# A hybrid decoder trunk: indexer score products placed between the weight products of the second recurrent projection chunk, and every selection round placed in the gaps of VectorE

## What is computed

```python
h = rms_norm(x, norm_g[l])
proj = h @ w_in[l]
a_part, b_part, c_part, gate_part = split_cols(proj, ...)
o_a = dsa_mixer(a_q, a_k, a_v, a_qi, a_ki, a_wi, bias_a)      # top-k attention
o_b = gated_deltanet_mixer(b_qkv, b_a, b_b, conv_w, ...)      # recurrent
o_c = nsa_mixer(c_q, c_kv, c_g, ...)                          # compressed, selected, window
merged = g_a * (y_a @ wb_a) + g_b * (y_b @ wb_b) + g_c * (y_c @ wb_c)
x = x + merged @ w_out[l]
```

```python
idx_logits = jnp.einsum('bqhd,bsd->bqhs', qib, k_idx) * (IDX_DIM ** -0.5)       # IDX_HEADS = 8, IDX_DIM = 64
score = jnp.einsum('bqh,bqhs->bqs', wb * (IDX_HEADS ** -0.5), jax.nn.relu(idx_logits))
score = jnp.where(key_pos[None, None, :] <= t[None, :, None], score, NEG_INF)
_, sel = lax.top_k(score, topk)                                                 # topk = 128
```

## Time and profile before

| | us |
|---|---|
| median of 3 runs | 659.43 (658.7 to 665.79) |
| the profiled execution, its own time | 658.73 |
| its span (first to last instruction) | 656.9 |
| mean granted TensorE clock | 0.982 of full |

### The profile page before, as it was taken

The page is one execution under the profiler, slowest core; times in us unless marked ns, Lnnn a source line. Parts: engine busy times, 40 slices in busy tenths (PEclk is TensorE's granted clock), DMA queues, the critical chain, the costliest instruction groups (busy, mean ns, idle before and its releaser), DMA issues.

```text
span 656.9 us, 9683 instructions
## 1 busy us (share of the span) xinstructions
PE 606.8 (92%) x3643; PEld 383.7 (58%) x3643; DVE 372.4 (57%) x820; ACT 324.5 (49%) x565; POOL 222.3 (34%) x161
## 2 busy tenths in 40 slices
PE   3869999999999997999999899999999999899998
PEld 2424557655347754777677677655666677333443
DVE  6401485443799989887878757342324453577411
ACT  4535645336656857622613415445766767243510
POOL 0133453522016466222630521226431233142520
PEclk9998999999999899999999999979999999899999
DMA  9244775543013332120210210202031111162411
GB/s 320 62 124 112 157 112 168 155 134 112 2 33 101 110 97 65 32 65 1 78 52 1 65 32 1 77 21 62 8 94 32 66 65 33 32 221 74 145 59 48
DMA packets 31167, 53.03 MB, mean 81 GB/s; under 512 B 2743, under 2 KB 13201, under 8 KB 31121
## 3 DMA queue, kind: packets, MB, share of 16 engines
q1 hardware_dynamic: 30961, 52.27, 27.8%
q10 hardware_dynamic: 160, 0.14, 0.1%
HBM read 49.98 MB, written 2.42 MB: 80 GB/s over the span
## 4 chain that ended last, share of the span: by engine, by line
PE 67%; DVE 17%; ACT 4%; issue 4%; POOL 3%; DMA 2%; SPq 2%; DVEq 0%; ACTq 0%; POOLq 0%
PE bank L1510 11%; PE bank L1512 10%; PE bank L1511 10%; PE bank L1682 8%; PE bank L1750 5%; PE bank L1752 5%; PE bank L1754 5%; DVE work L1246 3%; PE bank L1858 3%; DMA stage<-in_w_in 2%; PE bank L1546 2%; POOL w_lo L500 2%; DVE early L1154 2%; PE bank L1666 2%; PE bank L1877 2%
## 5 line engine op out<-in xcount | busy, mean ns | idle before, releaser
L500 POOL TENSOR_TENSOR w_lo<-stage,w_hi 128x1024 f16<-128x1024 f32 (+4 forms) x76 | 149.8, 1973 | 243.1 <-ACT w_hi L713 243.1
L1682 PEld LDWEIGHTS bank<-work 128*128 128x128 f32 x616 | 75.3, 192 | 17.6 <-DVEq L1221 12.5
L1682 PE MATMUL bank<-work 128*128 128x128 f32 x616 | 79.8, 278 | 5.5 <-DVEq L1221 5.1
L713 ACT ACTIVATE w_hi<-stage 128x1024 f16<-128x1024 f32 (+4 forms) x76 | 74.5, 981 | 16.8 <-issue 12.4
L705 ACT ACTIVATE stage<-stage,small 128x512 f32<-128x512 f32 (+4 forms) x120 | 73.6, 662 | 7.7 <-DMA stage<-in_w_in 7.7
L1750 PE MATMUL bank<-hT_hi,w_hi 128*128 128x512 f16 x192 | 74.5, 388 | 1.7 <-PE bank L1754 0.9
L1752 PE MATMUL bank<-hT_lo,w_hi 128*128 128x512 f16 x192 | 74.1, 386 | 0.4
L1754 PE MATMUL bank<-hT_hi,w_lo 128*128 128x512 f16 x192 | 74.0, 386 | 0.3
L1510 PE MATMUL bank<-w_hi,hT_hi 128*128 128x260 f16 (+4 forms) x192 | 62.4, 325 | 9.4 <-POOL w_lo L500 5.7
L1511 PE MATMUL bank<-w_lo,hT_hi 128*128 128x260 f16 (+4 forms) x192 | 62.3, 324 | 0.0
L1512 PE MATMUL bank<-w_hi,hT_lo 128*128 128x260 f16 (+4 forms) x192 | 62.2, 324 | 0.0
(11 more groups left out here) (296 smaller groups left out, 1132.3 us busy)
## 6 DMA issues: line engine op xcount, KB each, us to landing
stage<-in_w_in SPq DMA_DIRECT2D x40, 512.0 KB, 3.6
stage<-in_c_phi_w SPq DMA_DIRECT2D x8, 512.0 KB, 3.8
stage<-in_w_branch SPq DMA_DIRECT2D x8, 512.0 KB, 3.7
stage<-in_w_out SPq DMA_DIRECT2D x8, 512.0 KB, 3.9
stage<-in_w_in SPq DMA_DIRECT2D x8, 260.0 KB, 2.8
strips<-rel_rows SPq DMA_DIRECT2D x8, 256.0 KB, 6.8
late<-in_x SPq DMA_DIRECT2D x1, 2048.0 KB, 9.6
out_x<-late SPq DMA_DIRECT2D x8, 256.0 KB, 2.0
```

The lines of the kernel that those rows point to most:

```text
L500: gp.tensor_tensor(piece_view(w_lo[:, k % PAIRS, :], c), piece_view(stage[:, piece_at[c, j] % STAGES, :], c), piece_view(w_hi[:, k % PAIRS ...
L713: nc.scalar.activation(piece_view(w_hi[:, k % PAIRS, :], c), full, ACT.Copy).then_inc(hi_ready, 1)
L1682: ins = mm(ps[:, h * P:(h + 1) * P], lhs(h), rhs(h), start=True, stop=True)
```

## The change

The 24 score products go into the first seven slices' gaps of B1, six per output tile (after slices 1 to 6), and through the gate banks (`X`, with semaphores of its own). ReLU buffers go from two to four. ScalarE does the six ReLUs of a tile, then drains the tile of B1; VectorE does six sums, then one convolution. `topk(1)` joins the generator of the other two: TOPK_A is 20 steps, TOPK_B is 10, and the third next stands in `between_steps` after the copy of z. The transpose "kcT" and its square root move behind B3, and the order of GpSimd's masks and squares follows.

```diff
-TOPK_A, TOPK_B = 16, 6
+TOPK_A, TOPK_B = 20, 10
+
+IDX_PER_TILE = 6
...
-        relu_buf = [late[:, 640:1152], late[:, 1152:1664]]
+        relu_buf = [late[:, 640 + 512 * n:1152 + 512 * n] for n in range(4)]
...
+        idx_units = [(q, h) for q in range(1, NT) for h in range(IDX_HEADS)]
+        X = Uses(banks[2:4], idx_units)
...
                 if c == CH_B1:
-                    for m in range(4):
+                    diagonal(1)
+                    for m in range(3):
                         squares_b(m)
+                    diagonal(2)
+                    diagonal(3)
+                if c == CH_B3:
+                    squares_b(3)
...
+            def relus(t):
+                for n in range(IDX_PER_TILE * t, IDX_PER_TILE * (t + 1)):
+                    if n >= 4:
+                        act.wait_ge(relu_used, n - 3)
+                    L = P * (idx_units[n][0] + 1)
+                    act.wait_ge(x_filled, X.filled(idx_units[n]))
+                    nc.scalar.activation(relu_buf[n % 4][:, 0:L], X.bank(idx_units[n])[:, 0:L], ACT.Relu).then_inc(x_drained, 1)
...
-            drain_chunk(CH_B1, "B1", lambda t: qkvT[:, 4 + t, 3:T + 3], between=lambda t: silus(t, {0: (0, 1), 1: (2, 3)}))
-            drain_chunk(CH_B3, "B3", lambda t: raw_b[:, t, 0:260], 260)
+            for t in range(4):
+                relus(t)
+                drain(("B1", t), qkvT[:, 4 + t, 3:T + 3], scale=1.0 / W_SCALE)
+                follow(CH_B1, t)
+                silus(t, {1: (0,), 2: (1,), 3: (2,)})
+            def after_b3(t):
+                silus(t, {0: (3,)})
+                if t == 1:
+                    sqrt("kc", ss_kc[0:N_CMP, :], 1)
+
+            drain_chunk(CH_B3, "B3", lambda t: raw_b[:, t, 0:260], 260, between=after_b3)
...
+            for t in range(4):
+                score_sums(t)
+                conv(t)
...
-            for m in range(4):
-                conv(m)
-            for _ in topk(1):
-                pass
...
             def topk_later():
+                yield from topk(1)
                 yield from topk(2)
                 yield from topk(3)
...
                     if l < 3 or next(extras, "end") == "end":
                         next(topk_last, None)
                         if not late_in_level:
+                            next(topk_last, None)
                             next(topk_last, None)
...
+            def index_scores(n):
+                q, h = idx_units[n]
+                L, r = P * (q + 1), 64 * (h % 2)
+                if X.free((q, h)) > 0:
+                    pe.wait_ge(x_drained, X.free((q, h)))
+                mm(X.bank((q, h))[:, 0:L], qiT[r:r + 64, h // 2, (q - 1) * P:q * P], kiT[r:r + 64, 0:L],
+                   start=True, stop=True).then_inc(x_filled, 1)
+
+            def within_b1(t, k):
+                if (t, k) == (0, 1):
+                    pe.wait_ge(hid_ready, 1)
+                    pe.wait_ge(v_drained, V.filled("kiT"))
+                if 1 <= k <= IDX_PER_TILE:
+                    index_scores(IDX_PER_TILE * t + k - 1)
...
+            project(CH_B1, "B1", False, between=between_b1, within=within_b1)
+            project(CH_B3, "B3", True)
             T_IN.wait(pe, "kc")
             transposes("kcT", [raw_c0[0:N_CMP, 0, 0:128]], N_CMP)
-            project(CH_B3, "B3", True)
+            pe.wait_ge(x_drained, X.filled(idx_units[-1]))
```

More of the change, by code:

```diff
@@ L231, in trunk @@
         s_names = [(c, t) for c in ("C0", "C1", "A0", "QI", "A2", "B0") for t in range(4)]
-        s_names += [("idx", q, h) for q in range(1, NT) for h in range(IDX_HEADS)]
         s_names += [(c, t) for c in ("B1", "B3", "B4", "B2") for t in range(4)]
@@ L271, in trunk @@
         g_filled, g_drained = sem("gate_banks_filled"), sem("gate_banks_drained")
+        x_filled, x_drained = sem("index_banks_filled"), sem("index_banks_drained")
         w_loaded = [sem(f"weights_loaded{n}") for n in range(STAGES)]
@@ L543, in _, with diagonal @@
                     hold(gp.tensor_copy(level_masks[:, :, :], mask_halves))
-            for q in range(1, NT):
+            def diagonal(q):
                 gp.wait_ge(score_ready, q)
@@ L1097, in _, with score_sums @@
                 twin(("ak", h), k_a[:, h, 0, :], k_a[:, h, 1, :], R_AK)
[L1099 to L1104, removed]
+            def score_sums(t):
+                for n in range(IDX_PER_TILE * t, IDX_PER_TILE * (t + 1)):
+                    q, h = idx_units[n]
+                    ve.wait_ge(x_drained, X.filled((q, h)))
+                    r, wi = relu_buf[n % 4][:, 0:P * (q + 1)], raw_a2[:, q, 64 + h:65 + h]
                     if h == 0:
@@ L1108, in _ @@
                         ins = ve.scalar_tensor_tensor(scores[q - 1], r, wi, scores[q - 1], ALU.mult, ALU.add)
-                    n += 1
                     ins.then_inc(relu_used, 1)
-                    ve.wait_ge(relu_used, n)
-                ve.nop().then_inc(score_ready, 1)
+                    ve.wait_ge(relu_used, n + 1)
+                    if h == IDX_HEADS - 1:
+                        ve.nop().then_inc(score_ready, 1)
             def conv(m):
@@ L1660, in _, with between_b1 @@
             pe.nop().then_inc(hid_filled, 1)
[L1661 to L1673, removed]
+            def index_scores(n):
+                q, h = idx_units[n]
+                L, r = P * (q + 1), 64 * (h % 2)
[9 more added lines that the diff above has]
+                    index_scores(IDX_PER_TILE * t + k - 1)
+            def between_b1(t):
+                if t == 0:
+                    ps = v_bank("cmpkv")
+                    for v in range(2):
+                        for h in range(2):
+                            ins = mm(ps[0:N_CMP, 64 * v:64 * v + 64], hidT[:, 2 * v + h, :], phi2[:, 2 * v + h, :],
+                                     start=h == 0, stop=h == 1)
+                    ins.then_inc(v_filled, 1)
+            project(CH_B1, "B1", False, between=between_b1, within=within_b1)
+            project(CH_B3, "B3", True)
             T_IN.wait(pe, "kc")
             transposes("kcT", [raw_c0[0:N_CMP, 0, 0:128]], N_CMP)
-            project(CH_B3, "B3", True)
+            pe.wait_ge(x_drained, X.filled(idx_units[-1]))
             def four(name, lhs, rhs, ring_=None):
```

## The result

| | before | changed |
|---|---|---|
| median of 4 executions each | 662.61 us (658.7 to 667.11) | 680.1 us (679.79 to 680.46) |
| profiled execution, its span | 658.73 us, 656.9 us | 680.05 us, 678.3 us |
| mean granted TensorE clock in it | 0.982 | 0.975 |

The ratio is 1.0254 [1.0195, 1.0312]: the changed kernel is slower, by 2 to 3%. I had forecast 669.5 us, +10.8; measured between the two profiled executions it is +21.3. The kernel before has executions at 658 to 660 us and others at 665 to 667 us, and the one profiled is of the shorter kind; against the longer ones the change costs only some 14 us.

What follows compares the result with a forecast made beforehand. TensorE was taken to set the time except where it waits, with VectorE setting the loop's pace. The terms 1.8 + 1.9 + 0.5 + 0.5 + 6.1 = +10.8 us on 658.73 gave 669.5 us, range 659 to 675.

Steps and rivals of the forecast that it cites:

- (a): Score products moved into B1: 20.3 us of stream time and excursions come for 18.5 that go, +1.8 us.
- real work: Old score-product stretch before B1: its 19.0 us said to be no hole, since the products in it are work.
- (b): Last tile of B1: TensorE waits 1.9 us for a ReLU queued behind ScalarE's split of B3's piece 3.
- (c): Around B3 and B4: fourth SiLU and square root stand ahead of ScalarE's last split of B4's weights, +0.5 us.
- (d): Selection steps around the decay (TOPK_A, TOPK_B): 0.9 us more, 0.4 hidden by a VectorE wait, +0.5 us.
- (e): Delta rule's loop: 15.3 us of added selection steps and masks, less 9.2 absorbed by VectorE's waits, +6.1 us.
- waits of 9.6 us together: Loop: sixteen VectorE waits for TensorE, at merges, state products and cumulative sums, that can take some added steps.
- The check on one level: Loop, level 4 of chunk 1: with three steps on 512 keys, 4.9 + 0.76 = 5.6 us.
- TensorE paces the loop: Rival: TensorE's gate products set the loop's pace, so added steps cost near zero there; 663.4 us, chance 0.12.
- Smooth interleaving: Rival: score products in B1 cost only their columns (-3.0) and the last tile's wait doesn't come; 662.8 us, chance 0.12.
- Faster: Rival: smooth products and a TensorE-paced loop together, and 4 us less from low clock; 652.7 us, chance 0.07.
- The clock falls in the loop: Rival: TensorE's longer waits in the loop bring 1.2 GHz episodes in three chunks, +5.5 us; 675.0 us, chance 0.12.

Runs made afterwards that it cites:

- e4: The changed kernel with score products in pairs, even and odd head back to back, after slices 1, 3 and 5 of each B1 tile: 666.08 us.
- e1: The changed kernel with each score product on all 128 rows instead of half of them, same columns and instructions: 667.29 us.
- e2: The changed kernel with ScalarE's split of B3's piece 3 moved from before the last B1 tile's ReLUs to after its third product's ReLU: 673.5 us.
- e3: The kernel before with only the selection part of the change, score products left where they were: 674.91 us.
- e7: The changed kernel, lone score products and splits kept, with selection steps placed as in e5 (two, not three, after the copy of z): 671.52 us.
- e5: e4 with the piece 3 split later and selection steps placed where VectorE has time, 48 in the loop: 661.5 us.

## Why the prediction was wrong

The direction was right, and all terms but one place of low clock were on the list; the sum came out at half of what was measured.

**(a) Score products, +1.8 predicted, +4.2 measured.** The form of the sum held: stream time plus an excursion per product. That the 18.5 us of the old stretch were "real work" did not: 7 of them were waiting, as e4 shows, though for lone products that leaves the sum as it is. The failed term is the excursion, 0.2 us taken and 0.30 measured (e1 against the changed kernel). I had taken a value between the 33-row products' 0.18 and a bound that counts the load of 128 columns of weights; the bound was the answer.

**(b) The wait in the last tile, +1.9 predicted, 1.75 measured.** The working holds (e2 removes the wait by moving the split). What I left out is what stood behind it: 4.4 us lost at 1.2 GHz in B1. I had this mechanism as a rival, but in the loop, where the earlier trace rows had shown it. In the loop TensorE's waits grew, to 7.2 us in 11 of them, and the clock stayed at 1.00. What this place has and e1 and e2 lack is both: a wait of 1.75 us and, next to it, the half-row products. Take away either, and the clock stays full there; with the products in pairs (e4) it falls for 3.4 us. Why it takes both is open. These are single traces, in which everything behind the edit has also moved by microseconds, and the same score products ran at either clock in e3 and in the kernel before; so a matter of timing isn't excluded. For the reading speaks that e7, with the wait and the lone products, has the low stretch again. The Trainium skill's rule that I had put beside that rival, in "TensorE: Matmul & The Clock Gate", section "A second HAM failure mode: psum-queue depth-cycling", speaks of frequent micro-idles; the loop's eleven waits of up to 1.6 us at a clock of 1.00 don't bear it out here.

**(c) Around B3 and B4, +0.5.** The whole from B3 to B2 is +0.6, with some 2 us of low clock at its start and as much gone from B4. e1 and e4 have the low stretch in B4 as the kernel before has it and none in B3, and take 27.7 us for 27.4: the term is +0.3.

**(d) Steps around the decay, +0.5 predicted, +0.6 measured.**

**(e) The loop, +6.1 predicted, +9.4 measured (e3 +9.35, e7 back to +0.3).** What came was nearly right: 15.3 us of steps predicted (the terms as printed add up to 15.5), and 14.7 us more busy time by the windows, with 2.0 us more of the short gaps that each instruction brings. What failed is "waits of 9.6 us together" that can take 9.2 of it. VectorE's waits in the loop shrank by 7.3 us only (26.5 to 19.2, added up from its timeline). The merges' fell from 14.4 to 7.9, as I had it. The six at the sums and the state products stayed, 2.5 us. Those at the sums are round trips through a bank that the merge itself frees, and the steps stand ahead of the merge; those at the state products kept their size in the same way. Of the 9.2 us that makes 1.9 us of the miss (9.2 less 7.3); a mask instruction of 0.99 us where its neighbour of the same form takes 0.36 is 0.6; some 0.8 us is spread and not assigned. The check on one level, 5.6 us for level 4 of chunk 1, was short as well: it is 342.99 to 348.62, 5.63 us, for level 5, but 6.50 for level 4, which got the two mask instructions. No run has 66 steps in the loop at other places, so how much of the loss is their number and how much the third step behind the copy of z isn't shown.

**The rivals.** "TensorE paces the loop" fell with e3. "Smooth interleaving" fell with e1: smooth it is, but only for products on all rows. "Faster" needed both. "The clock falls in the loop" gave a time between the forecast and the measured one, but named the wrong place.

In numbers: +21.4 measured less +10.8 predicted is 10.6. Of this 2.4 is (a), 4.4 the clock in B1, 3.3 the loop, 0.6 the rest after the last copy; together 10.7, and the small terms and rounding take 0.1 back.

## What to carry to other kernels

A short product that uses part of the rows should not stand alone in a stream of full-row products: here each change to it and back cost 0.30 us, and two of them on different row halves cost no more than one. An engine's wait is room for more work only if what it waits for doesn't hang on the engine's own previous instruction; follow the wait to its start before taking it off a sum. When work is moved onto an engine that is full in a stretch, look for what the other engines have queued behind it, as the 5.80 us wait for the keys in e5.

## What the runs showed of the hardware that I had not expected

- A pair of float32 products of 64 rows and 512 columns, on both halves of the rows, takes 1.06 us between float16 products, as a single one does (e4). In the old stretch the same four instructions spanned 1.61 us, with 0.53 us idle ahead, the second product starting 0.49 us after the first.
- TensorE ran at 1.2 GHz for some 13.6 us in the changed kernel, busy nearly all of the time, after 1.75 us of waiting. The same wait with full-row products (e1) and the same products without the wait (e2) left the clock full there; the same wait with the products in pairs (e4) gave 3.4 us of it.
- In e3 the stretch of half-row products ran at 1.2 GHz for 20 us with TensorE 19.95 us busy, where the profiled execution of the kernel before has it at full clock with the same instructions.
